# Two transformer layers on unnormed rows: root mean squares applied behind the products, rows handled tile by tile, parameter and band loads moved to other queues

## What is computed

```python
x = x + gate_f * rmsnorm(moe, g_post_ffn)                 # end of the expert block
for i in range(2):
    x = x + 0.5 * swiglu_ffn(rmsnorm(x, ffn1_norm[i]), ffn1_wi[i], ffn1_wo[i])
    u = rmsnorm(x, mix_norm[i])
    z = u @ w_in[i]                                       # 4360 columns: heads, gates
    hA = mlstm(...); hB = sliding_window_attention(...)   # both from z
    mixed = sigmoid(ga) * (sigmoid(mo) * hA @ w_a[i]) + sigmoid(gb) * (hB @ w_b[i])
    x = x + mixed @ w_out[i]
    x = x + 0.5 * swiglu_ffn(rmsnorm(x, ffn2_norm[i]), ffn2_wi[i], ffn2_wo[i])
    gate = sigmoid(rmsnorm(x, ple_norm[i]) @ w_ple_gate[i])
    x = x + gate * (p[i] @ w_ple[i])
# rmsnorm(x, g) = x * rsqrt(mean(x*x) + 1e-6) * g, one factor per row
# swiglu_ffn(h) = (silu(h @ wg) * (h @ wu)) @ wo, 2816 hidden columns
```

## Time and profile before

| | before |
|---|---|
| median of 3 runs | 2549.64 us (2548.65 to 2554.34) |
| profiled execution, its time | 2546.16 us |
| profiled execution, its span | 2544.4 us |
| TensorE matmul busy | 1967.4 us (77%) |
| VectorE busy | 889.1 us (35%) |
| ScalarE busy | 660.2 us (26%) |
| mean granted TensorE clock | 0.873 of full |

### The profile page before, as it was taken

The page is one execution under the profiler, slowest core; times in us unless marked ns, Lnnn a source line. Parts: engine busy times, 40 slices in busy tenths (PEclk is TensorE's granted clock), DMA queues, the critical chain, the costliest instruction groups (busy, mean ns, idle before and its releaser), DMA issues.

```text
span 2544.4 us, 33208 instructions
## 1 busy us (share of the span) xinstructions
PE 1967.4 (77%) x12475; PEld 1372.9 (54%) x12475; DVE 889.1 (35%) x1220; ACT 660.2 (26%) x925; POOL 30.9 (1%) x56
## 2 busy tenths in 40 slices
PE   7886655565656565564999888899979988889997
PEld 4554111111111111112999866799869987668995
DVE  1234000000000000001666645666545656565664
ACT  2111000000000000002444443444434444434443
POOL 0000000000000000000000000000000000000000
PEclk8997877877787777777999997899989999889998
DMA  9961999999999999997555532355435544234551
GB/s 353 335 244 67 398 428 427 427 428 428 427 427 427 427 428 427 428 428 303 191 172 191 159 106 83 116 198 179 155 127 178 198 149 150 73 127 158 173 181 50
DMA packets 173475, 659.76 MB, mean 259 GB/s; under 512 B 9859, under 2 KB 106924, under 8 KB 142388
## 3 DMA queue, kind: packets, MB, share of 16 engines
q1 hardware_dynamic: 166316, 648.71, 65.8%
q10 hardware_dynamic: 6696, 7.40, 1.0%
q0 software_dynamic: 352, 2.11, 0.2%
HBM read 655.55 MB, written 2.64 MB: 259 GB/s over the span
## 4 chain that ended last, share of the span: by engine, by line
issue 91%; PE 5%; DMA 2%; POOL 1%; SPq 0%; DVE 0%; ACTq 0%; POOLq 0%; ACT 0%; PEldq 0%; DVEq 0%; PEld 0%
PE PS L1384 2%; DMA ring<-in_w_ada 1%; PE PS L1633 1%; PE PS L1393 1%; PE PS L1344 1%; POOL arena L524 0%; SPq L407 0%; PE PS L1867 0%; DMA mod_rows<-wide 0%; POOL ms L524 0%; POOL head_ms L524 0%; PE PS L1425 0%; DVE arena L178 0%; POOLq L523 0%; PE PS L1443 0%
## 5 line engine op out<-in xcount | busy, mean ns | idle before, releaser
L178 DVE TENSOR_TENSOR units<-ring,units 128x1024 fp32r<-128x1024 f32 (+2 forms) x384 | 466.4, 1215 | 356.7 <-ACT units L178 330.7
L1633 PE MATMUL PS<-hT_split,units 128*128 128x256 f32 x4416 | 549.3, 285 | 7.4 <-DVE units L178 7.3
L1633 PEld LDWEIGHTS PS<-hT_split,units 128*128 128x128 f32 x4416 | 545.8, 193 | 14.3 <-issue 7.5
L178 ACT ACTIVATE units<-ring 128x1024 fp32r<-128x1024 f32 (+2 forms) x384 | 404.0, 1052 | 544.0 <-PE PS L1633 527.4
L178 ACT ACTIVATE arena<-PS 128x256 f32<-128x256 f32 (+3 forms) x251 | 119.5, 476 | 1045.2 <-PE PS L1603 319.7
L178 DVE SCALAR_TENSOR_TENSOR arena<-arena,PS 128x256 f32<-128x256 f32 (+2 forms) x142 | 80.6, 568 | 886.2 <-ACT arena L178 545.9
L1595 PE MATMUL PS<-moe_ring,arena 128*32 128x512 f32 x1280 | 215.5, 810 | 154.1 <-DMA moe_ring<-in_w_gate_e 79.8
L1633 PE MATMUL PS<-units,hT_split 128*128 128x512 f32 (+2 forms) x1344 | 311.8, 392 | 16.3 <-DVE hT_split L178 11.0
L1633 PEld LDWEIGHTS PS<-units,hT_split 128*128 128x128 f32 x1344 | 255.4, 193 | 64.8 <-issue 11.0
L1633 PE MATMUL PS<-units,hid_split 128*128 128x512 f32 x1056 | 255.4, 391 | 0.0
L1595 PEld LDWEIGHTS PS<-moe_ring,arena 128*32 128x32 f32 x1280 | 41.1, 130 | 320.0 <-DMA moe_ring<-in_w_gate_e 121.8
(11 more groups left out here) (186 smaller groups left out, 988.2 us busy)
## 6 DMA issues: line engine op xcount, KB each, us to landing
moe_ring<-in_w_gate_e SPq DMA_DIRECT2D x48, 2048.0 KB, 25.8
ring<-in_w_down_e SPq DMA_DIRECT2D x48, 2048.0 KB, 26.3
ring<-in_ffn_wi SPq DMA_DIRECT2D x88, 1024.0 KB, 5.4
ring<-in_w_up_e SPq DMA_DIRECT2D x32, 2048.0 KB, 26.2
moe_ring<-in_w_up_e SPq DMA_DIRECT2D x32, 2048.0 KB, 26.3
ring<-in_ffn_wo SPq DMA_DIRECT2D x44, 1024.0 KB, 4.9
ring<-in_w_in SPq DMA_DIRECT2D x40, 1024.0 KB, 5.4
ring<-in_w_gate_e SPq DMA_DIRECT2D x16, 2048.0 KB, 27.2
```

Source lines behind the costliest of these rows:

```text
L178: return instruction(*args, **kwargs)
L1633: passes = [mm(out, lhs[i], rhs[j], start=start and i + j == 0, stop=stop and i == 1, **flags) for i, j in ((0, 0), (0, 1), (1, 0))]
```

## The change

In the layers no normed rows are written any more. TensorE turns x itself, tile 0 as soon as its addition is done, and the products are made from unnormed rows (with the gain). The root is made on GpSimd beside the products, as ms and, times 0.25 or 0.5, as ms_scaled. Where rows stand on partitions the factor is applied as a scale of one value per partition when the product leaves PSUM; where rows stand along the free axis (FFN hidden, mqkT) TensorE makes a row of roots in bank 7 with two 32-bit products, VectorE copies it, and products are multiplied with it. The last four units of w_out and w_ple_gate are taken tile by tile. The parameters go to SyncE's queue, between the fills of steps 9 and 10 of the first FFN, the band to GpSimd's queue behind the roots of the first block; the two-tile additions, the expert block's end and the layer's end go tile by tile. Counters of several signals are merged. The diff, cut to its core:

```diff
-    def ffn(pos, wi, wo):
+    def layer_constants():
+        sp.dma_start(p_("ffn1"), a["ffn1_norm_2"][1 - l].rearrange("(p k) -> p k", k=KT)).then_inc(
+            S["gain_full"], 16)
+        for name in NORMS[1:]:
...
+        sp.dma_start(w_ple, a["w_ple_2"][l].rearrange("(j p) n -> p j n", p=P)).then_inc(S["ple_full"], 16)
...
-row_root("last", 0, ms_post[:, :])
+pool.wait_ge(S["skew_written"], 16)
+nc.gpsimd.dma_start(band, bass.AP(skew.tensor, P, [[3 * P - 1, P], [3 * P * P, SW_H], [1, TOK]])).then_inc(
+    S["band_full"], 16)
+for t in range(NT):
+    row_root(f"last{t}", 0, ms_post[:, t:t + 1])
+def scaled_root(name, scale, l):
+    inverse_root("mean_squares", squares_turn(name, l), ms[:, :], eps_rms, "row_roots")
+    nc.gpsimd.drain()
+    nc.gpsimd.tensor_tensor(ms_scaled[:, :], ms[:, :], scale, ALU.mult).then_inc(S["row_roots"], 1)
...
-square_sums(lambda t: two_banks(6 * t), ms_post, "combined", (1 + NQ, 1 + NQ))
-act.wait_ge(S["x_layer"], NT)
-act.wait_ge(S["skew_written"], 16)
-program.dma_start(band, bass.AP(skew.tensor, P, [[3 * P - 1, P], [3 * P * P, SW_H], [1, TOK]])).then_inc(
-    S["band_full"], 16)
+for t, (signal, turn) in enumerate((("combined_first", NQ), ("combined", 1 + NQ))):
+    act.wait_ge(S[signal], turn)
+    square_sum(two_banks(6 * t), t, ms_post, arena[:, 6 * D:7 * D])
...
-def norm(name, need, values, l, also=lambda: None):
-    square_sums(lambda t: x[:, t, :], ms, need, values)
-    also()
-    act.wait_ge(S["row_roots"], norm_turn(name, l))
-    activation(hn[:, 0, :], x[:, 0, :], ACT.Copy, scale=ms[:, 0:1]).then_inc(S["hn"], 1)
+def square_of(t, need, values):
+    act.wait_ge(S[need], values[t])
+    return activation(unread_rows, x[:, t, :], ACT.Square, scale=1.0 / 32, accum_out=ms[:, t:t + 1])
+def norm(name, need, values, l):
+    square_of(0, need, values)
+    norm_T_hi(name, l)
+    square_of(1, need, values).then_inc(S["mean_squares"], 1)
...
+def ffn_tanh(off, hidden, base, fills):
+    def sub(c, hidden, base, fills):
+        act.wait_ge(S["f_gate"], hidden + (c + 1))
+        activation(f_tanh[:, c % 2, :], f_act[:, c % 2, :], ACT.Tanh, scale=0.5).then_inc(S["f_tanh"], 1)
...
-    norm("ffn1", "x_layer", (NT * l + 1, NT * l + 2), l, lambda: program.dma_start(
-        p_("ffn1"), a["ffn1_norm_2"][l].rearrange("(p k) -> p k", k=KT)).then_inc(S["gain_full"], 16))
+    gate_up_hi(OFF_FFN1, 0, before, layer_fills)
     act.wait_ge(S["gain_full"], (l + 1) * 16)
...
+    norm("ffn1", "x_layer", (NT * l + 1, NT * l + 2), l)
+    gate_up_hi(OFF_FFN1, 1, before, layer_fills)
+    ffn_tanh(OFF_FFN1, l * 2 * FFN_SUBS, before, layer_fills)
...
-    norm_T_hi("mix", l)
     piece_hi(1)
-    piece_done(0)
-    activation(mqkT, PS[:, 0:4, 0:TOK], ACT.Copy).then_inc(S["mqkT"], 1)
+    act.wait_ge(S["row_roots"], scaled_turn("mix", l))
     piece_hi(2)
     piece_done(1)
-    activation(gate_rows, PS[:, 4:6, 0:2 * ML_H], ACT.Copy).then_inc(S["gate_rows"], 1)
-    activation(sq[:, :, 0:384], PS[:, 4:6, 2 * ML_H:2 * ML_H + 384], ACT.Copy).then_inc(S["sq_copied"], 1)
+    for t in range(NT):
+        last = activation(gate_rows[:, t, :], PS[:, 4 + t, 0:2 * ML_H], ACT.Copy, scale=ms[:, t:t + 1])
+    last.then_inc(S["z_copied"], 1)
+    for t in range(NT):
+        last = activation(sq[:, t, 0:384], PS[:, 4 + t, 2 * ML_H:2 * ML_H + 384], ACT.Copy,
+                          scale=ms[:, t:t + 1])
+    last.then_inc(S["z_copied"], 1)
...
-                       PS[:, (2, 4, 2, 0)[j] + t, :], ACT.Tanh, scale=0.5).then_inc(S["g_copied"], 1)
+                       PS[:, (2, 4, 2, 0)[j] + t, :], ACT.Tanh,
+                       scale=ms_scaled[:, t:t + 1]).then_inc(S["g_copied"], 1)
...
     norm_T_hi("mixed", l)
     halves_hi(stage_units(OFF_WO, 4, 4), D, before, layer_fills)
     gate_up_hi(OFF_FFN2, 0, before, layer_fills)
+    act.wait_ge(S["pT_ps"], l + 1)
+    activation(pT, PS[:, 4, :].rearrange("p (j n) -> p j n", j=2), ACT.Copy).then_inc(S["pT"], 1)
     norm("ffn2", "x_mix", (2 * l + 1, 2 * l + 2), l)
-    norm_T_hi("ffn2", l)
     gate_up_hi(OFF_FFN2, 1, before, layer_fills)
-    ffn_tanh(OFF_FFN2, before, layer_fills)
...
-    act.wait_ge(S["pT_ps"], l + 1)
-    activation(pT, PS[:, 0, :].rearrange("p (j n) -> p j n", j=2), ACT.Copy).then_inc(S["pT"], 1)
-    norm_T_hi("ple", l)
     halves_hi(stage_units(OFF_PLE, 4, 4), D, before, layer_fills)
-    act.wait_ge(S["unit_used"], before + LAYER_UNITS)
-    for t in range(NT):
-        activation(ga[:, t, :], two_banks(2 * t), ACT.Tanh, scale=0.5).then_inc(S["ple_tanh"], 1)
+    act.wait_ge(S["row_roots"], scaled_turn("ple", l))
+    for t in range(NT):
+        if t == 0:
+            act.wait_ge(S["rows_done"], rows_turn("ple", l))
+        else:
+            act.wait_ge(S["unit_used"], before + LAYER_UNITS)
+        activation(ga[:, t, :], two_banks(2 * t), ACT.Tanh, scale=ms_scaled[:, t:t + 1]).then_inc(
+            S["ple_tanh"], 1)
...
-    dve.wait_ge(S["row_roots"], norm_turn("last"))
-    for t in range(NT):
-        stt(hn[:, t, :], PS[:, apart * t:apart * t + 2, :].rearrange("p b n -> p (b n)"), ms_post[:, t:t + 1],
-            gate, ALU.mult, ALU.mult)
-    for t in range(NT):
-        tt(x[:, t, :], x[:, t, :], hn[:, t, :], ALU.add).then_inc(S[signal], 1)
+    for t in range(NT):
+        dve.wait_ge(S["mean_squares"], norm_turn(f"last{t}"))
+        tt(hn[:, t, :], PS[:, apart * t:apart * t + 2, :].rearrange("p b n -> p (b n)"), gate, ALU.mult)
+        dve.wait_ge(S["row_roots"], norm_turn(f"last{t}"))
+        last = stt(x[:, t, :], hn[:, t, :], ms_post[:, t:t + 1], x[:, t, :], ALU.mult, ALU.add)
+        last.then_inc(S[signal], 1)
...
+def row_of_roots(turn):
+    dve.wait_ge(S["root_row"], turn)
+    dve.run(V.tensor_copy, root_row, PS[:, 7, 0:TOK])
...
+        act_, gu = f_act[:, c % 2, :], f_gu[:, c % 2, :]
+        if c == FFN_SUBS - 1:
+            down_rest(off, c, base)
+        dve.wait_ge(S["unit_used"], base + (2 * off + gate_unit(c) + 2))
+        tt(act_, PS[:, 4 + c % 4, 0:TOK], root_row, ALU.mult).then_inc(S["f_gate"], 1)
+        tt(gu, act_, PS[:, 4 + c % 4, TOK:2 * TOK], ALU.mult)
+        if c < FFN_SUBS - 1:
+            down_rest(off, c, base)
         dve.wait_ge(S["f_tanh"], hidden + (c + 1))
-        act_ = f_act[:, c % 2, :]
-        stt(act_, f_tanh[:, c % 2, :], 1.0, PS[:, 4 + c % 4, 0:TOK], ALU.add, ALU.mult)
-        tt(act_, act_, PS[:, 4 + c % 4, TOK:2 * TOK], ALU.mult)
+        stt(act_, f_tanh[:, c % 2, :], 1.0, gu, ALU.add, ALU.mult)
         dve.run(V.tensor_copy, hid_split[:, 0, c % 2, :], act_)
         tt(hid_split[:, 1, c % 2, :], act_, hid_split[:, 0, c % 2, :].bitcast(F32),
            ALU.subtract).then_inc(S["f_hid"], 1)
         if c + 2 < FFN_SUBS:
             gate_up_rest(off, c + 2, base)
-        if c + 1 < FFN_SUBS:
-            down_rest(off, c + 1, base)
...
-def add_rows(scale, signal):
-    for t in range(NT):
-        stt(x[:, t, :], PS[:, 2 * t:2 * t + 2, :].rearrange("p b n -> p (b n)"), scale, x[:, t, :],
+def add_rows(name, scale, signal, l, off):
+    for t in range(NT):
+        if t == 0:
+            dve.wait_ge(S["rows_done"], rows_turn(name, l))
+        else:
+            dve.wait_ge(S["unit_used"], l * LAYER_UNITS + 2 * off)
+        stt(x[:, t, :], PS[:, 2 * t:2 * t + 2, :].rearrange("p b n -> p (b n)"), scale(t), x[:, t, :],
             ALU.mult, ALU.add).then_inc(S[signal], 1)
+by_root = lambda t: ms_scaled[:, t:t + 1]
...
-    norm("ffn1", l)
+    split_rest(2 * OFF_FFN1, gate_up_weights(POS_LAYER + OFF_FFN1, 0, 0), before)
     dve.wait_ge(S["gain_full"], (l + 1) * 16)
     norm_T_rest("ffn1", l)
-    for c in range(2):
-        gate_up_rest(OFF_FFN1, c, before)
+    split_rest(2 * OFF_FFN1 + 1, gate_up_weights(POS_LAYER + OFF_FFN1, 0, 1), before)
+    gate_up_rest(OFF_FFN1, 1, before)
+    row_of_roots(3 * l + 1)
...
-    piece_rest(0, 0, 3)
-    used_to(OFF_Z)
-    add_rows(0.25, "x_ffn1")
-    piece_rest(0, 3)
-    norm("mix", l)
+    piece_rest(0, 0, 2)
+    dve.wait_ge(S["row_roots"], scaled_turn("ffn1", l))
+    add_rows("ffn1", by_root, "x_ffn1", l, OFF_Z)
+    piece_rest(0, 2)
     norm_T_rest("mix", l)
     piece_rest(1)
+    row_of_roots(3 * l + 2)
+    dve.wait_ge(S["row_roots"], scaled_turn("mix", l))
+    used_to(OFF_Z + 2)
+    tt(mqkT, PS[:, 0:4, 0:TOK], root_row.unsqueeze(1).to_broadcast([P, 4, TOK]), ALU.mult).then_inc(
+        S["mqkT"], 1)
...
-    dve.run(V.tensor_copy, mva[:, :, :, 0:ML_DV], heads(PS[:, 2:4, :], ML_H)).then_inc(S["mva"], 1)
+    for t in range(NT):
+        last = ts(mva[:, t, :, 0:ML_DV], PS[:, 2 + t, :].rearrange("p (h d) -> p h d", h=ML_H),
+                  ms[:, t:t + 1], None, ALU.mult)
+    last.then_inc(S["mva"], 1)
...
+    add_rows("mixed", lambda t: 0.5, "x_mix", l, OFF_FFN2)
     gate_up_rest(OFF_FFN2, 0, before)
-    used_to(OFF_FFN2)
-    add_rows(0.5, "x_mix")
-    norm("ffn2", l)
     norm_T_rest("ffn2", l)
     gate_up_rest(OFF_FFN2, 1, before)
+    row_of_roots(3 * l + 3)
...
```

(82 more changed lines are left out.)

172 lines of the change are left out of this document (78 added, 94 removed).

## The result

The changed kernel takes 2520.18 us in the median of four runs (2513.77 to 2526.61), the kernel before 2550.1 in the same comparison: a ratio of 0.9878 [0.9853, 0.9904], about 30 us gained. Forecast were 2499 (2489 to 2515) and a gain of 50.9. The sign is right, the gain is 16 to 21 us short of the sum, and the time lies outside the range.

A forecast was written before the change was run, and what follows sets the result against it. TensorE was taken to bound the FFN, leaving the seams between stages to gain: 55.5 us less 3.6 and 1.0 gives 50.9, and 2549.64 - 50.9 = 2498.7, told as 2499 us, range 2489 to 2515.

The forecast's parts named there:

- experts to first FFN: From the experts' last product to the end of up(0) in the first FFN: 15.2 us gained by turning tile by tile.
- FFN to input projection, two: Seam between first FFN and input projection, in both layers: products start sooner, 4.2 us gained each, 8.4 in all.
- output projection to second FFN, two: Seam behind the output projection, in both layers: up(0) of the second FFN ends earlier, 4.2 us each, 8.4.
- FFN to gated embedding, two: Seam behind the second FFN, in both layers: gated embedding starts at 1828.1 instead of 1832.35, 4.2 us each, 8.4.
- layer end, once: From the first w_ple product to the next layer's up(0): 20.6 us instead of 33.1, gain 12.5.
- rows of roots, six: Added 32-bit products before up(1), piece 1 and up(1), 6 in all: 0.6 us each, 3.6 lost.
- scales and split copies, attention: Split tanh and value copies and scales behind piece 4: 0.5 us lost a layer, 1.0 in all.
- band among the experts: The band's 1 MB transfer on GpSimd's queue may meet the experts' weights: taken as 0, at most 3.1 us.
- second rival: Clock stays low behind the seams: 10 to 15 us lost, gain 38, time 2512; chance 12%.
- rival 4: FFN's inner chain of gate product, tanh and hidden values becomes the bound, stretching 88 substeps: slower, example 2675; chance 3%.
- Rival 3: More gained than counted, by a warm clock at the gated embedding and hidden roots: gain 58, 2491; chance 8%.
- Parameters: 12 issues on SyncE, 4.7 us in all, between fills in the first FFN, ScalarE losing 11: cost and gain 0.

The follow-up runs named there:

- e7: Changed kernel with the layer loops of VectorE and ScalarE written out and TensorE kept busy in the seams by products nothing reads: 2493.8 us, ratio 0.9758.
- e1: Changed kernel with 14 products of 128x512 a layer that nothing reads, put where TensorE otherwise waits: 2505.57 us, ratio 0.9835.
- e4: Kernel before the change with the band's transfer alone moved to GpSimd's queue, ahead of the first block's last root: 2549.47 us, ratio 0.9997.
- e2: Changed kernel with the loop over the two layers written out on VectorE and ScalarE: 2503.25 us, ratio 0.9828.
- e5: Changed kernel with the last four units of w_out and w_ple_gate taken unit by unit again, not tile by tile: 2518.13 us, ratio 0.9855.
- e6: Changed kernel with the parameters, except the next layer's gain, issued by ScalarE again at the first FFN's head: 2516.81 us, ratio 0.9847.
- e11: e7 plus twelve more unread products a layer, eight ahead of the attention's last softmax, four ahead of w_a's products: 2487.69 us, ratio 0.9743.

## Why the prediction missed, step by step

All in us, the forecast beside the profiled pair (from the stage table), and e7.

| term | forecast | measured | in e7 |
|---|---|---|---|
| experts to first FFN | 15.2 | 15.1 | 14.7 |
| FFN to input projection, two | 8.4 | 6.8 | 8.6 |
| output projection to second FFN, two | 8.4 | 7.6 | 9.1 |
| FFN to gated embedding, two | 8.4 | 7.6 | 8.5 |
| layer end, once | 12.5 | 9.5 | 12.9 |
| very end | 2.6 | 2.6 | 2.6 |
| rows of roots, six | -3.6 | -2.8 | |
| scales and split copies, attention | -1.0 | -2.5 | |
| low clock on the products, behind shortened seams | 0 | -3.9 | |
| low clock on the products, elsewhere | 0 | -6.6 | |
| sum over the layers | 50.9 | 33.4 | 57.1 |
| band among the experts | 0 | -1.3 | |
| first stretch, by chance | 0 | -9.9 | |

**The step that failed most** is "My sum has the clock up at the first products of each layer, since TensorE is idle only some 2 us at a stretch there, with transposes between", and that the sum had no term for the clock anywhere else either. The low clock on products cost 10.5 us. It is the excess over the kernel before of the first pieces (13.46 against 11.61 and the roots' 0.36: 1.5 twice), the pieces behind the wait (1.7 twice), the output projections (1.49, 0.72), the gated embeddings (0.60, 0.30) and the branches (-0.21, 1.27).

At the layer starts themselves it cost nothing. up(0) of layer 0 ran at full clock. In layer 1 its first 24 products ran at 0.50 for 2.8 us, but the second 24 had to wait 0.42 us more for VectorE's rest of unit 1; what was late there is the third step below.

The earlier trace rows had the sign: the clock was at 0.50 or 0.72 in the seams. I read it as something that a shorter seam removes. Where the change shortened a seam (first pieces, gated embeddings) the low clock now lies on the products or lies there longer; that is 3.9 of the 10.5 us. The other 6.6 lie behind idle stretches that are about as long as before: the wait for a unit's rest (2.64 us before, 2.70 now), the stretch ahead of the output projection (9.12 and 9.12, though the transposes in it now come in two parts) and the one ahead of the products with w_a (9.04 and 9.23). So "the seam lost its cover" explains the smaller part. That it is the clock, e1 shows; why it now falls on these products is open, and e4 shows it falling so in the kernel before as well.

My second rival gave 10 to 15 us, a gain of 38 and 2512, with 12%. Its total came true in the layers, its places only in part: it had 2.4 at each of two layer starts, where nothing was lost, and 1 to 2 at six other seams, where 6.1 was measured in all; the 3.3 behind the wait and the 1.1 in the branches it didn't have. That the total fits is partly luck.

**The second** is in the seams' chains. "VectorE makes two rests ... adds tile 0 ... and tile 1 ..." is right in its order and its operations, but I put the operations end to end with at most 0.15 between them, as the earlier trace rows shows for rests alone. In a loop over layers a wait value is computed first, and between the additions it is 0.47. This cost 0.9, 0.5 and 0.5 a seam; in e2 and e7 the marks are my numbers (6.2 for 6.3).

**The third** is "Then as at the first seam, 10.8 more" for the layer end. The jump costs VectorE 2.9 to 3.0 us; the kernel before has it as well (its branch at 1867.72, the next instruction at 1870.59), there hidden for the most part behind the root on GpSimd, which was done at 1869.85. I had cost an edit that removed the cover without naming what was under it. The Trainium skill has the rule, in Runtime: NRT & Kernel Launch, Instruction fetch mechanics: a taken branch whose target isn't loaded must fetch it first. The 3.0 us are in line with it (that they are the fetch was not tried apart), and I had not weighed it.

**The smaller ones.** Roots: 24 records took 3.6 us as I said, but each overlaps its neighbours; net 0.36 at the input projection and 0.51 in each FFN with its other additions, 2.8 in all. The attention's stretch lost 1.3 and 0.6 and not 0.5, among it small waits of 0.1 to 0.3 per head; what the low clock has in it wasn't separated. The FFN's inner chain (rival 4) didn't move: 181.76 in all four. Rival 3 was also added up wrongly: its parts as stated, 0.4 us at each gated embedding and the roots' 3.6, give a gain of 55.3 and not 58, nor the 60 at the low end of the range. Band: my 0 was 1.2, inside its bound. Rows by tile: I gave it no term of its own, and e5 shows it has none. Parameters: 0 as forecast, though by the cover of a seam that e6 shows to be gone in layer 0.

**The comparison's base.** The profiled execution before had the shortest first stretch of all 13 profiles (215.79), the one after the longest (225.65). The layers and the experts alone, 33.4 - 1.3 = 32.1 us, agree with the two medians' 30 and 35.

## What to carry to other kernels

When a seam shrinks, ask what the long seam was hiding: a loop's jump, a queue's issues, and the low clock that follows an idle TensorE. Don't let the clock stand at nothing in a sum because a seam gets shorter: here the low clock fell on products behind shortened seams and behind unchanged ones. TensorE products that nothing reads, in a free bank and shorter than the wait, kept it at 1.00 where they were put and were worth more than most of the seams. Judge a change of a few us by the distance between marks around it, not by two spans, if a stretch elsewhere varies by 10 us.

## What was not expected of the hardware

- The granted clock fell to 0.50 about 1 us after the products had begun (1401.23, and 0.50 from 1402.4 on), at a time when TensorE was fully busy; it came of the idle stretch ahead of these products, since it stayed away where e1 filled that. It fell too behind the 2.70 us idle ahead of the fifth piece; behind the same wait in the kernel before (2.64 us) it did so in one of four cases (e4, layer 0). With 24 products of 0.9 us a layer that nothing reads, and the loops written out, the mean granted clock was 0.98 instead of 0.95 (windows of the changed kernel and of e11, whose window begins some 15 us ahead of the layers):

```profile
1197.00:2522.00 1325.00, 1215.16 (x7448) 1089.15 (x7448) 822.12 (x1146) 567.57 (x736) 28.28 (x35) 0.95 0.45 151
```

```profile
1180.00:2486.00 1306.00, 1242.24 (x7616) 1091.82 (x7616) 823.47 (x1146) 570.49 (x742) 28.69 (x36) 0.98 0.47 157
```

- The jump back over a layer's program took 2.9 to 3.0 us on VectorE and a like idle time on ScalarE (2.95, [<-issue]), while the jump of the FFN's short inner loop shows in no substep.
- Waits whose value is computed from the loop's index left 0.30 and 0.47 us ahead of VectorE's two additions in a seam; with constants (e7) it was 0.17 and 0.10.
- Some DMA issues on ScalarE took 1.3 us instead of 0.4 (two of eleven in e6).
